# A two-layer transformer in one launch: block attention computes all values first, by rows of tokens, and then queries and keys two units a head

## The chip, the cores and the metric

The kernel runs on one core of one Trainium2 chip. The metric is the time on the device for one launch, in microseconds (us); it was measured in three runs. Besides, one execution was recorded by the profiler, and all durations here come from that one.

## The reference, cut to what matters

The reference is two transformer layers on 512 tokens of width 1024. Each layer is a gated feed-forward block, an attention block and a second feed-forward block, with norms before and after each. The change lies in the attention of the first layer (8 heads of 128). With 512 tokens in two blocks of 256 and every earlier block chosen, its block selection keeps all earlier blocks, so it is plain causal attention:

```
hn  = rms_norm(x, g[2])
qkv = (hn @ w_qkv).reshape(bsz, s_len, 3, A_HEADS, A_HEAD_DIM)     # 1024 x 3072
q   = apply_rope(qkv[:, :, 0], cos_h, sin_h)
k   = apply_rope(qkv[:, :, 1], cos_h, sin_h)
v   = qkv[:, :, 2]
p   = softmax(causal(q @ k.T * 128 ** -0.5))
mix = (p @ v) @ w_o
x   = x + rms_norm(mix, g[3])
```

All data is float32. The kernel keeps float32 accuracy by splitting every operand into a rounded part and a rest (`hi` and `lo`) and by three matmuls for each product: hi x hi, hi x lo, lo x hi.

## The kernel before

The program is written out engine by engine, with semaphores between them; nothing schedules it. Each engine goes strictly through its own list, so an instruction that waits holds up all behind it. TensorE (PE) computes; ScalarE (ACT) makes the hi parts and exponentials; VectorE (DVE) makes the lo parts, the softmax's maxima and normalisation and most evacuations of PSUM; GpSimd (POOL) adds the two halves of the rotary embedding; SyncE (SP) issues the loads of weights.

Weights come as *units* of 1024 x 128 (512 KB) into four slots: a load into `raw`, the hi part `wh` on ACT (`split`, L643), the lo part `wl` on DVE (`split`, L1178), and then 8 tiles of 3 matmuls on PE (`unit`, L1928), which signals `unit_done`. A unit's hi part waits until the unit four places earlier is done.

Activations lie transposed, features on partitions and tokens along the row: `xg` holds the normed input as hi and lo. In stage 1 the attention of the first layer takes 24 units in the order query, key, value of head 0, then of head 1, and so on. The first four units (query, key and value of head 0, query of head 1) are computed by `quad` (L1948): first for tokens 0 to 255, while the second half of `xg` is still being made, and then for tokens 256 to 511, each matmul with 256 columns. In between PE does the transposes for the norms (`mean`, `spread`). All later units have 512 columns.

A value unit gives the head's values transposed. DVE scales them into `tmp` (`evac_v`, L1624), PE turns them back in four 128 x 128 transposes (`value_transposes`, L2168), and `v_split` makes hi and lo parts in `vh` on ACT and DVE. A query or key is evacuated as two products with cosine and sine on DVE (`products`, L1502 and L1503), ACT exchanges the halves (L872), POOL adds, and ACT and DVE make the hi and lo parts (L881, L1507).

For each head `h` from 1 to 6 the loop of PE (L2273) has: the scores of head `h` (`scores`); seven transposes of the probabilities of head `h - 1` (pieces 0 and 1); the unit 3h+4; three more transposes (piece 2); the unit 3h+5; probabilities times values of head `h - 1` (`values`, L2151), whose third step waits until piece 2 has its lo part on DVE; the unit 3h+6; and the value transposes of head `h + 1`. DVE and ACT have their own lists for a head (L1655 and L1004): products, mask, lo parts of the probabilities, maxima, exponentials, normalisation. `out_proj` (L2175) holds the last heads and the first four units of the output projection, whose tiles for the heads already done fill PE meanwhile.

Of the kernel before, what the change touches and what calls it, by code (L numbers as in the profile page):

```python
# [11 lines left out]
P = 128  # L12
# [5 lines left out]
def yoco_kernel(nc: bass.Bass, x, norm_gains, ffn_w1, ffn_w3, ffn_w2, moba_w_qkv, moba_w_o, mla_w_dq,  # L18
# [130 lines left out]
    with ExitStack() as ctx:  # L149
# [129 lines left out]
        def vT_bank(n):  # L279

            return acc[3] if n else aux
# [79 lines left out]
        vT_psum = sem("vT_psum")  # L361
        v_hi = sem("v_hi")
# [52 lines left out]
        def values_of(n):  # L415

            return vh[:, n % 2, 0], vh[:, n % 2, 1]

# [34 lines left out]
        def _(sp):  # L453
# [85 lines left out]
            plain(U0[1], qkv, [HEADS * P * a + P * h for h in range(HEADS) for a in range(3)])  # L539
# [89 lines left out]
        def _(act):  # L629
# [279 lines left out]
            def v_split(n):  # L909
                act.wait_ge(vT_psum, n + 1)  # L910
                s.activation(values_of(n)[0], vT_bank(n)[:].rearrange("p (t d) -> p t d", d=P), COPY
                             ).then_inc(v_hi, 1)
# [61 lines left out]
            split(u + 4)  # L974
            split(u + 5)
            load_table(EXP)
            split(u + 6)
            split(u + 7)

            def exchanged(h, i):  # L980
                exchange(evacuated, r + 3 * h + i + 1, (rope_q, rope_k)[i])
# [6 lines left out]

            probT_zeros()
            for i in range(2):  # L990
                exchanged(0, i)
            for i in range(2):
                rotated(0, i)
            v_split(0)

            for i in range(2):
                exchanged(1, i)
            for i in range(2):
                rotated(1, i)
            softmax_exp(0)  # L1000
            v_split(1)
            split(u + 8)
            split(u + 9)
            for h in range(1, HEADS - 1):  # L1004
                exchanged(h + 1, 0)
                probT_split(h - 1, (0, 1))
                rotated(h + 1, 0)
                split(u + 3 * h + 7)
                if h == 1:
                    probT_split(h - 1, (2,))  # L1010
                softmax_exp(h)
                exchanged(h + 1, 1)
                if h > 1:
                    probT_split(h - 1, (2,))
                split(u + 3 * h + 8)
                rotated(h + 1, 1)
                o_split(h - 1)
                split(u + 3 * h + 9)
                v_split(h + 1)
            probT_split(HEADS - 2, (0, 1, 2))  # L1020
            softmax_exp(HEADS - 1)
            o_split(HEADS - 2)
# [147 lines left out]
        def _(dve):  # L1170
# [391 lines left out]
            def v_split(n):  # L1562
                dve.wait_ge(v_hi, n + 1)
                v_h, v_l = values_of(n)
                v.tensor_tensor(v_l, vT_bank(n)[:].rearrange("p (t d) -> p t d", d=P), f32(v_h),
# [58 lines left out]
            def evac_v(u_count, bank):  # L1624
                dve.wait_ge(unit_done, u_count)
                v.tensor_tensor(T[3][:], bank, Rb[:], ALU.mult).then_inc(evacuated, 1)

            def products(h, i):
                if h:
                    dve.wait_ge(part_lo, 2 * (h - 1) + i + 1)  # L1630
                rope_products(u + 3 * h + i + 1, att_banks[1][3 * h + i][:], cosR, sinR, (rope_q, rope_k)[i])
# [4 lines left out]
            products(0, 0)  # L1636
            products(0, 1)
            split(u + 6)
            evac_v(u + 3, acc[2][:])
            rotated(0, 0)  # L1640
            rotated(0, 1)
            products(1, 0)
            products(1, 1)
            split(u + 7)
            v_split(0)
            softmax_mask(0)
            softmax_max(0)
            evac_v(u + 6, att_banks[1][5][:])
            rotated(1, 0)
            rotated(1, 1)  # L1650
            softmax_norm(0)
            v_split(1)
            split(u + 8)
            split(u + 9)
            for h in range(1, HEADS - 1):  # L1655
                products(h + 1, 0)
                softmax_mask(h)
                probT_split(h - 1, (0, 1))
                softmax_max(h)
                rotated(h + 1, 0)  # L1660
                split(u + 3 * h + 7)
                if h == 1:
                    probT_split(h - 1, (2,))
                softmax_norm(h)
                products(h + 1, 1)
                if h > 1:
                    probT_split(h - 1, (2,))
                split(u + 3 * h + 8)
                rotated(h + 1, 1)
                o_split(h - 1)  # L1670
                split(u + 3 * h + 9)
                evac_v(u + 3 * h + 6, att_banks[1][3 * h + 5][:])
                v_split(h + 1)
            probT_split(HEADS - 2, (0, 1, 2))
            softmax_mask(HEADS - 1)
            softmax_max(HEADS - 1)
            softmax_norm(HEADS - 1)
            o_split(HEADS - 2)
# [197 lines left out]
        def _(pe):  # L1876
# [70 lines left out]

            def quad(st, xg0, n_post, n_pre, between=None):  # L1948
# [168 lines left out]
            def scores(n, rope=None):  # L2117
                if n:
                    pe.wait_ge(exp_ready, TS * n)
                for c in range(TS):  # L2120
                    if n == 0 and c == TS - 1:

                        pe.wait_ge(evacuated, R0[1] + 5)
# [13 lines left out]
            def prob_transposes(n, pieces):  # L2137
                pe.wait_ge(prob_ready, TS * (n + 1))
                for b in pieces:
                    if b == 1 and (n + 1) % HEADS:  # L2140
                        pe.wait_ge(v_lo, n + 2)
# [9 lines left out]
            def values(n):  # L2151

                if n:
                    pe.wait_ge(o_lo, n)
                else:
                    pe.wait_ge(evacuated, R0[1] + 7)
                pe.wait_ge(v_lo, n + 1)
# [10 lines left out]
            def value_transposes(n, r_count):  # L2168
                pe.wait_ge(evacuated, r_count)
                for j in range(TS):  # L2170
                    ins = t.transpose(vT_bank(n)[:, j * P:(j + 1) * P],
                                      (T[3] if n < HEADS else Rb)[:, j * P:(j + 1) * P], ident[:])
                ins.then_inc(vT_psum, 1)

            def out_proj(st, u, r, n, heads, last_scores):  # L2175
# [14 lines left out]
                pe.wait_ge(evacuated, att - 1)  # L2190
                pe.wait_ge(o_lo, last - 2)
                heads_done(0, 0, HEADS - 3)
                value_transposes(last, att)
                prob_transposes(last - 1, (0,))
                last_scores()
                prob_transposes(last - 1, (1,))
                pe.wait_ge(o_lo, last - 1)
                heads_done(0, HEADS - 3, HEADS - 2)
                prob_transposes(last - 1, (2,))
                pe.wait_ge(evacuated, att)  # L2200
                heads_done(1, 0, HEADS - 2)
                values(last - 1)
# [57 lines left out]
            quad(1, XG0[X_F0], N_F0, N_PRE1)  # L2260

            def qkv_unit(rr):
                unit(u + rr, att_dst(1, rr), from_x(xg))


            qkv_unit(4)
            qkv_unit(5)
            value_transposes(0, r + 3)
# [4 lines left out]
            for h in range(HEADS - 1):  # L2273
# [122 lines left out]
```

## Time and profile before

| | us |
|---|---|
| median of three runs (1861.65, 1863.51, 1863.53) | 1863.51 |
| the profiled execution | 1861.66 |
| its span, first to last instruction | 1859.7 |
| PE busy | 1842.6 |
| DVE busy | 1318.0 |
| ACT busy | 914.3 |
| POOL busy | 53.6 |

The busy times are of the span. A row of a matmul gives its full time through the array, which overlaps with the next one; what a matmul costs in a dense stretch is the distance between two starts. The granted clock of TensorE is given as a share of full speed, and is 1.00 in every stretch of this execution. The attention of the first layer lies between 364 us and 567 us.

### The profile page before, as it was taken

How to read it: one execution, taken by the hardware profiler on the slowest of the kernel's cores; microseconds unless marked ns; L12 is line 12 of the kernel's file. 1: busy time of each engine (PE TensorE's matmuls, PEld its weight loads, DVE VectorE, ACT ScalarE, POOL GpSimd, SP SyncE). 2: the span in 40 equal slices, each digit the busy share in tenths (PEclk: the TensorE clock that was granted, in tenths of full speed). 3: DMA queues.
4: the chain of work that ended last, by engine and by line, in shares of the span. 5: the costliest groups of instructions: out<-in, count | busy, mean ns of one | idle time of the engine just before them, and what ended most of it. 6: DMA issues, size and time to landing. Idle time of an engine off the chain costs nothing.

```text
span 1859.7 us, 31170 instructions
## 1 busy us (share of the span) xinstructions
PE 1842.6 (99%) x12175; PEld 1693.9 (91%) x12175; DVE 1318.0 (71%) x1742; ACT 914.3 (49%) x1386; POOL 53.6 (3%) x51
## 2 busy tenths in 40 slices
PE   8999999999999999999999999999999999999999
PEld 7899988988889899998898999989988898999888
DVE  6888862487656888882288888822888488888623
ACT  6455552355545545562255555622666464455522
POOL 0000000011100000000000000000000000000000
PEclk9999999999999999999999999999999999999999
DMA  6244343232223333333323343333221232343331
GB/s 183 80 113 113 91 115 102 79 90 72 77 57 102 91 91 106 97 104 106 108 57 108 91 113 104 102 98 104 63 63 57 69 91 84 99 112 105 109 102 47
DMA packets 339464, 174.64 MB, mean 94 GB/s; under 512 B 11070, under 2 KB 337836, under 8 KB 339372
## 3 DMA queue, kind: packets, MB, share of 16 engines
q1 hardware_dynamic: 338656, 172.25, 33.0%
q8 instruction: 65, 1.06, 0.2%
q10 hardware_dynamic: 716, 1.11, 0.2%
q14 instruction: 27, 0.22, 0.0%
HBM read 171.24 MB, written 2.10 MB: 93 GB/s over the span
## 4 chain that ended last, share of the span: by engine, by line
PE 85%; DVE 9%; ACT 3%; issue 2%; DMA 0%; POOL 0%; DVEq 0%; SPq 0%; ACTq 0%
PE acc L1881 19%; PE acc L1882 19%; PE acc L1883 19%; PE duo L1881 9%; PE duo L1883 9%; PE duo L1882 9%; DVE wl L1175 2%; DVE xg L1220 1%; DVE mx L1534 1%; PE acc L2147 1%; DVE probT L1555 1%; ACT prob L889 1%; DVE y L1240 1%; ACT wh L641 0%; DVE xT L1247 0%
## 5 line engine op out<-in xcount | busy, mean ns | idle before, releaser
L1881 PE MATMUL acc<-xg,wh 128*128 128x256 f32 (+1 forms) x1040 | 340.4, 327 | 2.4 <-DVE xg L1220 1.0
L1883 PE MATMUL acc<-xg,wl 128*128 128x256 f32 (+1 forms) x1040 | 336.9, 324 | 0.0
L1882 PE MATMUL acc<-xg,wh 128*128 128x256 f32 (+1 forms) x1040 | 336.8, 324 | 0.0
L1175 DVE TENSOR_TENSOR wl<-raw,wh 128x1024 fp32r<-128x1024 f32 (+2 forms) x198 | 228.9, 1168 | 126.5 <-ACT wh L641 126.2
L1882 PE MATMUL acc<-hT,wh 128*128 128x512 f32 (+1 forms) x704 | 255.2, 363 | 0.0
L1881 PE MATMUL acc<-hT,wh 128*128 128x512 f32 (+1 forms) x704 | 255.2, 363 | 0.0
L1883 PE MATMUL acc<-hT,wl 128*128 128x512 f32 (+1 forms) x704 | 255.2, 362 | 0.0
L641 ACT ACTIVATE wh<-raw 128x1024 fp32r<-128x1024 f32 (+2 forms) x198 | 194.4, 1011 | 116.4 <-PE acc L1883 71.8
L1881 PEld LDWEIGHTS acc<-xg,wh 128*128 128x128 f32 x1040 | 197.7, 190 | 20.5 <-issue 3.1
L1883 PEld LDWEIGHTS acc<-xg,wl 128*128 128x128 f32 x1040 | 197.7, 190 | 15.8
L1882 PEld LDWEIGHTS acc<-xg,wh 128*128 128x128 f32 x1040 | 197.9, 190 | 14.9
L730 ACT ACTIVATE tmp<-tmp 128x512 f32<-128x512 f32 x88 | 55.5, 631 | 225.6 <-DVE tmp L1437 130.9
L775 ACT ACTIVATE wh<-raw 128x1024 fp32r<-128x1024 f32 x128 | 134.7, 1055 | 48.7 <-PE duo L1883 47.9
L1881 PEld LDWEIGHTS acc<-hT,wh 128*128 128x128 f32 x704 | 132.9, 189 | 20.7
L1883 PEld LDWEIGHTS acc<-hT,wl 128*128 128x128 f32 x704 | 132.9, 189 | 20.6
L1882 PEld LDWEIGHTS acc<-hT,wh 128*128 128x128 f32 x704 | 132.9, 189 | 20.5
L1881 PE MATMUL duo<-xg,wh 128*128 128x256 f32 (+1 forms) x528 | 151.5, 287 | 0.0
L1882 PE MATMUL duo<-xg,wh 128*128 128x256 f32 (+1 forms) x528 | 151.1, 286 | 0.0
L1883 PE MATMUL duo<-xg,wl 128*128 128x256 f32 (+1 forms) x528 | 151.1, 286 | 0.0
L1407 DVE TENSOR_TENSOR wl<-raw,wh 128x1024 fp32r<-128x1024 f32 x128 | 150.9, 1217 | 0.2 <-ACT wh L775 0.2
L1881 PE MATMUL duo<-tx,wh 128*128 128x256 f32 x512 | 144.9, 283 | 0.0
L1882 PE MATMUL duo<-tx,wh 128*128 128x256 f32 x512 | 144.9, 283 | 0.0
(283 smaller groups left out, 4175.6 us busy)
## 6 DMA issues: line engine op xcount, KB each, us to landing
raw<-in_ffn_w_dram SPq DMA_DIRECT2D x238, 512.0 KB, 4.2
raw<-in_ffn_w_dram SPq DMA_DIRECT2D x32, 384.0 KB, 3.4
raw<-in_moba_w_qkv_dram SPq DMA_DIRECT2D x24, 512.0 KB, 3.8
raw<-in_moba_w_o_dram SPq DMA_DIRECT2D x8, 512.0 KB, 3.8
raw<-in_mla_w_o_dram SPq DMA_DIRECT2D x8, 512.0 KB, 3.7
xin<-in_x_dram SPq DMA_DIRECT2D x4, 512.0 KB, 5.4
raw<-in_mla_w_dq_dram SPq DMA_DIRECT2D x4, 512.0 KB, 3.9
raw<-in_mla_w_uq_dram SPq DMA_DIRECT2D x8, 256.0 KB, 2.9
```

The costliest lines, as they stand in the source:

```text
L641: s.activation(wh[:, slot, 0:tiles], raw[:, slot, 0:tiles], COPY).then_inc(w_hi, 1)
L730: s.activation(T[1][:], src, SILU).then_inc(silu_ready, 1)
L775: s.activation(dst, src, COPY).then_inc(w_hi, 1 + (i == 2))
L889: s.activation(prob_of(n, c), sco[bank][:, o:o + (c + 1) * P], EXP, bias=nmx[:, c:c + 1], scale=A_SCALE if n < HEADS else qscale[:, c:c + ...
L1175: v.tensor_tensor(wl[:, slot, 0:tiles], raw[:, slot, 0:tiles], f32(wh[:, slot, 0:tiles]), ALU.subtract).then_inc(w_lo, 1)
L1220: v.scalar_tensor_tensor(out=dst[:, 1, m, cols], in0=xT[:, m, cols], scalar=gains[:, gcol + m:gcol + m + 1], in1=f32(dst[:, 0, m, cols]), ...
L1240: v.tensor_tensor(y[:, a:b, half(e)], y[:, a:b, half(e)], norm_bank[e][:, half(e)].unsqueeze(1).broadcast_to([P, b - a, HALF]), ALU.mult). ...
L1407: v.tensor_tensor(dst, src, f32(high), ALU.subtract).then_inc(w_lo, 1 + (i == 2))
L1534: ins = v.tensor_reduce(mx[:, c:c + 1], sco[bank][:, o:o + (c + 1) * P], AX_X, ALU.max)
L1881: t.matmul(dst, w_h, m_h, start=start, stop=False, skip_group_check=onto)
L1882: t.matmul(dst, w_h, m_l, start=False, stop=False, skip_group_check=onto)
L1883: return t.matmul(dst, w_l, m_h, start=False, stop=stop, skip_group_check=onto)
```

## The change

Two things change in stage 1, and no others.

The eight value units are computed first, for all heads, and by rows of tokens: a matmul now takes 128 tokens of `xg` as its stationary operand and 512 columns of the value weights, four heads, as its moving one (`values_product`). The result has tokens on partitions, as `values` wants it, and no transposes are left. A unit now holds two of the eight feature tiles for four heads, loaded in one DMA. `all_values` does heads 0 to 3 for token blocks 0 and 1, then 2 and 3, and heads 4 to 7 in the same way. The results lie in all eight PSUM banks, four at a time; ACT writes the hi part with the token's norm factor as its scale (`values_hi`), DVE the lo part in one instruction (`values_lo`), both into `oT`, where each head's output later takes the place of its values.

After that come queries and keys, two units a head, for heads 0 and 1 before the first scores and then two heads ahead. The loop of a head has two units instead of three. The lists of ACT and DVE for a head are written anew, and `out_proj` has a form of its own for this stage (`moba_heads`), into which heads 5 to 7 fall.

```diff
-        for st, special in ((1, {4: sco[2], 5: acc[0], 6: aux}), (5, {KQ: sco[1], KQ + 1: sco[2]})):
+        for st, special in ((1, dict(enumerate((*acc, *sco, aux, *acc)))), (5, {KQ: sco[1], KQ + 1: sco[2]})):
...
+            def values_product(dst, slot, k, c, start, stop):
+                (x_h, x_l), cols = from_x(xg, slice(c * P, (c + 1) * P))(k), slice(VG * (k % 2), VG * (k % 2 + 1))
+                dst = dst[:].rearrange("p (h d) -> p h d", d=P)
+                t.matmul(dst, x_h, wh[:, slot, cols], start=start, stop=False)
+                t.matmul(dst, x_h, wl[:, slot, cols], start=False, stop=False)
+                return t.matmul(dst, x_l, wh[:, slot, cols], start=False, stop=stop)
+
+            def all_values(xg0, n_post, n_pre):
...
+                for e in range(2):
+                    for k in range(KD):
+                        if e == 0:
+                            pe.wait_ge(w_lo, u + k // 2 + 1)
+                        pe.wait_ge(xg_ready, xg0 + KD * e + k + 1)
+                        for c in range(HT * e, HT * (e + 1)):
+                            ins = values_product(att_banks[1][c], k // 2, k, c, k == 0, k == KD - 1)
...
+                        if (e, k) == (1, 4):
+                            mean(n_pre)
+                        if (e, k) == (1, 7):
+                            spread(n_pre)
...
 PE, the loop over heads:
-            for h in range(HEADS - 1):
+            for h in range(2):
+                qk_unit(h, 0)
+                qk_unit(h, 1)
+            for h in range(HEADS - 2):
                 moba_scores(h)
                 if h:
                     prob_transposes(h - 1, (0, 1))
-                    qkv_unit(3 * h + 4)
+                qk_unit(h + 2, 0)
+                if h:
                     prob_transposes(h - 1, (2,))
-                    qkv_unit(3 * h + 5)
                     values(h - 1)
-                if h + 2 < HEADS:
...
-                    qkv_unit(3 * h + 6)
-                if h + 2 < HEADS:
-                    value_transposes(h + 1, r + 3 * h + 6)
+                qk_unit(h + 2, 1)
...
+                def moba_heads():
+                    last_scores(last - 1)
+                    prob_transposes(last - 2, (0, 1))
...
+                    heads_done(0, 0, HEADS - 4)
+                    prob_transposes(last - 2, (2,))
+                    values(last - 2)
...
+                    heads_done(1, 0, HEADS - 4)
+                    last_scores(last)
+                    prob_transposes(last - 1, (0, 1))
+                    pe.wait_ge(o_lo, last - 1)
+                    heads_done(0, HEADS - 4, HEADS - 2)
+                    prob_transposes(last - 1, (2,))
+                    values(last - 1)
+                    heads_done(1, HEADS - 4, HEADS - 2)
```

The new list of ACT for a head (the removed lines have the old order, with three units a head):

```diff
+            for h in range(HEADS):
+                if h:
+                    probT_split(h - 1, (0, 1))
+                if h + 1 < HEADS:
+                    for i in range(2):
+                        rotated(h + 1, i)
+                softmax_exp(h)
+                if h:
+                    probT_split(h - 1, (2,))
+                for i in range(2):
+                    if h + 2 < HEADS:
+                        exchanged(h + 2, i)
+                    if i and h:
+                        o_split(h - 1)
+                    if h + 1 < HEADS:
+                        split(u + 14 + 2 * h + i)
```

And the new list of DVE for a head:

```diff
+            for h in range(HEADS):
                 softmax_mask(h)
+                if h:
+                    probT_split(h - 1, (0, 1))
                 softmax_max(h)
+                if h + 1 < HEADS:
+                    for i in range(2):
+                        rotated(h + 1, i)
+                softmax_norm(h)
+                if h:
+                    probT_split(h - 1, (2,))
+                for i in range(2):
+                    if h + 2 < HEADS:
+                        products(h + 2, i)
+                    if i and h:
+                        o_split(h - 1)
+                    if h + 1 < HEADS:
+                        split(u + 14 + 2 * h + i)
```

On PE, the place is behind the three transposes of piece 2 of a head. Before, a whole unit (24 matmuls from `xg`) stood there; here are its first rows:

```order
1829 L2147 MATMUL acc<-ident,prob_odd_104 128x128 x3
1830 L1881 MATMUL acc<-xg,wh 128x512
1831 L1882 MATMUL acc<-xg,wh 128x512
1832 L1883 MATMUL acc<-xg,wl 128x512
1833 L1881 MATMUL acc<-xg,wh 128x512
```

After the change the product of probabilities and values (`probT` and the values in `oT`) follows at once:

```order
1800 L2210 MATMUL acc<-ident,prob 128x128 x3
1801 L1899 MATMUL duo<-probT,oT 128x512
1802 L1900 MATMUL duo<-probT,oT 128x512
1803 L1901 MATMUL duo<-probT,oT 128x512
1804 L1899 MATMUL duo<-probT,oT 128x384
1805 L1900 MATMUL duo<-probT,oT 128x384
1806 L1901 MATMUL duo<-probT,oT 128x384
1807 L1899 MATMUL duo<-probT,oT 128x256
```

The unit that stood between has moved away: of a head's three units one lies ahead of the transposes and one behind the product.

On DVE, the place is the stretch ahead of a head's mask (the instruction on `duo` with `mask`) and behind it. `wl` is the lo part of a weight unit, `rope_k` and `tmp` the rotary products, `oT<-duo` the lo part of a head's output. Before, for a head in the middle:

```order
254 L1175 TENSOR_TENSOR wl<-raw,wh 128x1024
255 L1507 TENSOR_TENSOR kh<-rope_k_102,kh 128x512
256 L1560 TENSOR_TENSOR oT<-duo,oT 128x512
257 L1175 TENSOR_TENSOR wl<-raw,wh 128x1024
258 L1626 TENSOR_TENSOR tmp_64<-acc,Rb 128x512
259 L1565 TENSOR_TENSOR vh<-acc,vh 128x512
260 L1502 TENSOR_TENSOR tmp_62<-acc,sinR 128x512
261 L1503 TENSOR_TENSOR tmp_61<-acc,cosR 128x512
262 L1525 TENSOR_TENSOR duo<-duo,mask 128x128 x4
263 L1555 TENSOR_TENSOR probT<-acc,probT 128x512
```

And now:

```order
236 L1523 TENSOR_TENSOR rope_k_101<-acc,sinR 128x512
237 L1524 TENSOR_TENSOR rope_k_102<-acc,cosR 128x512
238 L1581 TENSOR_TENSOR oT<-duo,oT 128x512
239 L1196 TENSOR_TENSOR wl<-raw,wh 128x1024
240 L1546 TENSOR_TENSOR duo<-duo,mask 128x128 x4
241 L1576 TENSOR_TENSOR probT<-acc,probT 128x512
242 L1576 TENSOR_TENSOR probT<-acc,probT 128x384
243 L1555 TENSOR_REDUCE mx<-duo 128x1 x4
```

The products of the key's unit, which is the last one ahead of the scores on PE, now stand ahead of the mask, and the output's and one unit's lo part stand between the two.

## Rows read from the trace of the kernel before

**Rows 1.** The page: busy share of PE, and its granted clock in 40 slices.

```profile
PE 1842.6 (99%) x12175; PEld 1693.9 (91%) x12175; DVE 1318.0 (71%) x1742; ACT 914.3 (49%) x1386; POOL 53.6 (3%) x51
...
PEclk9999999999999999999999999999999999999999
```

**Rows 2.** Timeline of PE: start, duration, instruction; a 512-column matmul, then 256.

```profile
566.60 0.39 PE L1883 MATMUL duo<-oT,wl 128*128 128x512 f32 x1
566.83 0.28 PE L1881 MATMUL acc<-oT,wh 128*128 128x256 f32 x1
566.94 0.28 PE L1882 MATMUL acc<-oT,wh 128*128 128x256 f32 x1
```

**Rows 3.** Timeline of PE over one head of the loop (h = 5).

```profile
496.99 0.60 PE L2171 MATMUL acc<-ident,tmp 128*128 128x128 f32 x4
...
499.36 0.93 PE L2147 MATMUL acc<-ident,prob 128*128 128x128 f32 x7
...
505.59 0.49 PE L2147 MATMUL acc<-ident,prob 128*128 128x128 f32 x3
...
511.39 0.39 PE L1881 MATMUL duo<-probT,vh 128*128 128x512 f32 x1
...
512.63 0.38 PE L1881 MATMUL duo<-probT,vh 128*128 128x256 f32 x1
...
513.45 0.40 PE L1881 MATMUL acc<-xg,wh 128*128 128x512 f32 x1
...
518.90 0.60 PE L2171 MATMUL acc<-ident,tmp 128*128 128x128 f32 x4
```

**Rows 4.** Timeline of DVE over one head (h = 4).

```profile
476.91 0.68 DVE L1502 TENSOR_TENSOR tmp<-acc,sinR 128x512 f32<-128x512 f32 x1
...
478.11 0.88 DVE L1525 TENSOR_TENSOR duo<-duo,mask 128x128 f32<-128x128 f32 x4
480.23 1.15 DVE L1555 TENSOR_TENSOR probT<-acc,probT 128x512 fp32r<-128x512 f32 x2 [1.24 <-ACT probT L897]
481.30 1.67 DVE L1534 TENSOR_REDUCE mx<-duo 128x1 f32<-128x128 f32 x4
483.01 0.17 DVE L1539 TENSOR_SCALAR nmx<-mx 128x4 f32<-128x4 f32 x1
...
485.40 0.18 DVE L1546 RECIPROCAL rsums<-psums 128x4 f32<-128x4 f32 x1 [0.49 <-ACT prob L889]
485.61 1.27 DVE L1549 TENSOR_SCALAR prob<-prob,rsums 128x128 f32<-128x128 f32 x4
...
490.01 0.62 DVE L1555 TENSOR_TENSOR probT<-acc,probT 128x256 fp32r<-128x256 f32 x2 [1.93 <-ACT probT L897]
```

**Rows 5.** Timeline of ACT over the same head.

```profile
478.23 1.28 ACT L872 ACTIVATE tmp<-tmp 64x512 f32<-64x512 f32 x2 [1.95 <-DVE tmp L1503]
...
483.22 0.37 ACT L889 ACTIVATE prob<-duo,nmx 128x128 f32<-128x128 f32 x1 [0.72 <-DVE nmx L1539]
...
485.15 0.21 ACT L889 ACTIVATION_READ_ACCUMULATOR prob<-duo,nmx 128x1 f32 x1
...
491.71 0.60 ACT L907 ACTIVATE oT<-duo 128x512 fp32r<-128x512 f32 x1 [0.26 <-PE duo L1883]
492.21 1.06 ACT L641 ACTIVATE wh<-raw 128x1024 fp32r<-128x1024 f32 x1
```

**Rows 6.** Timeline of DVE: last square sum of the norm before attention.

```profile
383.97 0.42 DVE L1295 SCALAR_TENSOR_TENSOR sqs<-sqs 128x256 f32<-128x256 f32 x1
```

**Rows 7.** Timeline of PE at the program's start.

```profile
6.05 1.09 PE L2249 MATMUL duo<-ident,xin 128*128 128x128 f32 x4 [6.05 <-DMA xin<-in_x_dram]
...
7.11 2.77 PE L2249 MATMUL duo<-ident,xin 128*128 128x128 f32 x12
10.89 0.36 PE L1881 MATMUL acc<-xg,wh 128*128 128x256 f32 x1 [1.01 <-DVE xg L1220]
```

**Rows 8.** Windows: busy time (count) by engine, granted clock, DMA share, GB/s.

```profile
8.00:10.00 2.00, 1.88 (x9) 1.48 (x7) 1.67 (x4) 1.79 (x4) 0.00 (x0) 1.00 1.11 358
```

More of the change, by code:

```diff
@@ L415, in values_of, with values_part @@
         def values_of(n):
+            if n < HEADS:
+                return tuple(oT[:, a, n].rearrange("p (t d) -> p t d", d=P) for a in range(2))
             return vh[:, n % 2, 0], vh[:, n % 2, 1]
+        def values_part(i, a):
+            g, c = divmod(i, TS)
+            return oT[:, a, VG * g:VG * (g + 1), c * P:(c + 1) * P]
         def o_of(n, a):
@@ L538, in _ @@
             qkv = kpn(moba_w_qkv[0])
-            plain(U0[1], qkv, [HEADS * P * a + P * h for h in range(HEADS) for a in range(3)])
+            for i in range(V_UNITS):
+                g, j = divmod(i, KD // 2)
+                slot_free(U0[1] + i)
+                sp.dma_start(raw[:, i % SLOTS].rearrange("p (k h) n -> p k (h n)", k=2),
+                             qkv[:, 2 * j:2 * j + 2, (2 * HEADS + VG * g) * P:(2 * HEADS + VG * (g + 1)) * P]
+                             ).then_inc(raw_full[i % SLOTS], 16)
+            plain(U0[1] + V_UNITS, qkv, [HEADS * P * a + P * h for h in range(HEADS) for a in range(2)])
             plain(U0[1] + 3 * HEADS, kpn(moba_w_o[0]), range(0, D, P))
@@ L987, in rotated @@
                 part((qh, kh)[i][:, 0], (rope_q, rope_k)[i][1][:])
+            split(u + 4)
+            split(u + 5)
+            load_table(EXP)
+            for i in range(TS):
+                values_hi(i)
+            split(u + 6)
+            split(u + 7)
+            for i in range(TS, TS + HT):
+                values_hi(i)
+            for w in range(8, 11):
+                split(u + w)
             probT_zeros()
+            for i in range(TS + HT, 2 * TS):
+                values_hi(i)
+            split(u + 11)
             for i in range(2):
@@ L1630, in products @@
                     dve.wait_ge(part_lo, 2 * (h - 1) + i + 1)
-                rope_products(u + 3 * h + i + 1, att_banks[1][3 * h + i][:], cosR, sinR, (rope_q, rope_k)[i])
+                rope_products(u + V_UNITS + 2 * h + i + 1, att_banks[1][V_RES + 2 * h + i][:], cosR, sinR,
+                              (rope_q, rope_k)[i])
             def rotated(h, i):
                 part(2 * h + i, (qh, kh)[i], (rope_q, rope_k)[i][1])
-            products(0, 0)
-            products(0, 1)
+            for i in range(TS):
+                values_lo(i)
@@ new lines, in _ @@
+            for i in range(TS, TS + HT):
+                values_lo(i)
+            for w in range(8, 11):
+                split(u + w)
+            for i in range(TS + HT, 2 * TS):
+                values_lo(i)
+            split(u + 11)
+            for i in range(2):
+                products(0, i)
+            for i in range(2):
+                rotated(0, i)
+            for i in range(2):
+                split(u + 12 + i)
+                products(1, i)
+            for h in range(HEADS):
@@ L1669, in _ @@
[L1669 to L1678, printed above, removed]
+                if h + 1 < HEADS:
+                    for i in range(2):
+                        rotated(h + 1, i)
@@ L1679, in _ @@
+                softmax_norm(h)
+                if h:
+                    probT_split(h - 1, (2,))
+                for i in range(2):
+                    if h + 2 < HEADS:
[4 more added lines that the diff above has]
+                        split(u + 14 + 2 * h + i)
             probT_split(HEADS - 1, (0, 1, 2))
@@ L2259, in _, with qk_unit @@
             u, r = U0[1], R0[1]
[L2260 to L2268, printed above, removed]
+            all_values(XG0[X_F0], N_F0, N_PRE1)
+            def qk_unit(h, i):
+                rr = V_RES + 2 * h + i
+                unit(u + V_UNITS + 2 * h + i, att_dst(1, rr), from_x(xg))
             def moba_scores(h):
```

169 lines of the change are left out of this document (79 added, 90 removed).

## The prediction

> **What bounds the kernel now.** I read the page first: PE is busy for 99% of the span, at a granted clock of full speed in all slices [rows 1]. Nothing that shortens another engine's work can help by itself. The change has to take work from PE, and it must not make PE wait. So the second view is PE's timeline. In a dense stretch a 512-column matmul costs 0.227 us from start to start (0.23 in the row) and a 256-column one 0.12, so two halves cost slightly more than one whole [rows 2]. A 128x128 transpose costs 0.11: seven take 0.93 and four 0.60, and the difference is three of them [rows 3].
>
> One head of the loop takes 518.90 - 496.99 = 21.91 us without a gap [rows 3]. Its parts: value transposes with the change of shape 0.44; scores 1.93 (to 499.36); seven transposes 0.77; a unit 5.46; three transposes 0.33 (from 505.59); a unit 5.47; probabilities times values 2.06 (511.39 to 513.45); a unit 5.45. The third view is the timeline of DVE and ACT over a head, which tells how long the softmax takes from scores to normalised probabilities. These engines idle now and then, which costs nothing while PE has a unit in hand.
>
> **PE's own work.** The value units keep their 192 matmuls of 512 columns, with the operands' roles swapped; I take 0.227 for them too. `quad`'s 192 halves (four units x 8 tiles x 3 x 2) become 96 whole: 192 x 0.12 - 96 x 0.227 = 1.2 us less. The eight groups of four value transposes go: 8 x 0.44 = 3.5 us less [rows 3]. Together -4.7 us. The 32 lo and hi parts of values are off PE's path.
>
> **The value stage.** `mean` for the norm ahead of attention stood behind 24 + 12 halves of the second token half in the order before; now it stands behind five feature tiles, that is 5 x 6 x 0.227 = 6.8 us, and the first half is 0.6 us shorter. PE comes to it at about 383.4. DVE's last square sum ends at 383.97 + 0.42 = 384.39 [rows 6], and DVE's chain up to there is not moved: 1.0 us of waiting. Later, the third unit of heads 4 to 7 gets its lo part behind the norm's factors, both tables and four `values_lo` on DVE, about 395.3: the norm's factors come to DVE when PE is through the first group, 389.6, then 0.7 + 2 x 0.6 for factors and tables, 4 x 0.6 for the lo parts, 1.13 for the unit and some 0.2 of handing over. PE wants it after four feature tiles of the second group, 389.5 + 5.4 = 394.9: 0.4 us. Some 0.3 us of waits of that kind are there before, so I book +1.1.
>
> **A head in the new loop.** Without waits it would take 21.91 - 5.45 - 0.44 = 16.0 us. But DVE and ACT have a chain that is longer than PE's cover. I count from t = 0, where PE ends the key's unit and starts the scores of head h. The durations are those of rows 4 and 5, an op of 512 columns on DVE counting 0.60 to the next one (two from 476.91 to 478.11).
> - The key's two products on DVE: PE's end is seen 0.2 later, then 0.60 + 0.68: to 1.5. Before, the mask had only a query's products ahead of it, whose unit had ended long before.
> - ACT exchanges the halves (1.28): to 2.8. Then the output's hi part, which follows it in ACT's list (0.49 to the next [rows 5]), to 3.3; the unit's hi part, 1.06: to 4.4.
> - DVE's lo part of that unit, 1.13: to 5.5. The mask, 0.93: to 6.5 (scores were ready at 2.1, so all that stands ahead of it counts).
> - Lo parts of the earlier head's pieces 0 and 1, 1.07 (480.23 to 481.30): to 7.5. Maxima 1.71: to 9.25. Scaled maxima, then ACT's exponentials, from 483.01 to 483.22 to 485.36: 2.35, to 11.6.
> - Reciprocal and normalisation, 485.40 to 486.80: 1.4, to 13.0. Lo part of piece 2, 0.62 [rows 4]: to 13.65.
>
> PE comes to that piece much earlier. Scores, seven transposes, the query's unit and three transposes take 8.5 us; the first two steps of `values` (511.39 to 512.6, [rows 3]) 1.2: PE stands at 9.7 before the third step and can start it at about 13.75. That is a wait of 4.05 us in every head. Before, a whole unit of 5.47 us lay between the three transposes and `values` and hid it, and in DVE's list the lo part of piece 2 came at 490.01, just in time even so. Behind PE's wait stand the rest of `values` (0.8) and the key's unit (5.45), whose end starts the next head's chain, so nothing is won back: a head takes 20.0 us instead of 16.0. The pattern holds for h = 1 to 5 (h = 0 has no `values`): 5 x 4.05 = +20.2 us.
>
> **The last heads.** For head 6 the scores, seven transposes, half of one output tile (12 matmuls, 2.7 us instead of a unit's 5.4), three transposes and two steps bring PE to 7.0; the chain is the same, 13.75: 6.7 us. For head 7 nothing stands ahead of the mask. Counted from the start of its scores: scores 1.9, mask, lo parts, maxima, exponentials, normalisation and piece 2 take up to 10.7; PE's own work (scores, transposes, 6 matmuls of the output projection 1.4, three transposes, two steps) is done at 5.8: 4.9 us. Some 0.3 of small waits are there before. Together +11.3.
>
> **Sum.** -4.7 + 1.1 + 20.2 + 11.3 = +27.9 us.
>
> **The clock after a wait.** This is the cost that the trace of before hardly shows, since there PE waits longer than 1.01 us only at the start. After 6.05 us without work PE's twelve transposes took 2.77 us, which is (2.77 - 0.27) / 11 = 0.227 each instead of 0.11; then, after a wait of 1.01 us, 256-column matmuls went at full pace from 10.89 on [rows 7]. The window's granted clock reads 1.00 all the same [rows 8], so half speed may hide behind that figure. Sixteen transposes at twice their price make 1.9 us. A wait of 6.7 us is longer than the one that showed this, so I count one such loss, +2.0. Those of 4.05 and 4.9 lie between 1.01 and 6.05; nearest is the 6.05, but for these I take nothing in the sum and keep 6 x 2.0 = 12 us for the range; at the low end the clock costs nothing anywhere. The Trainium skill, in "TensorE: Matmul & The Clock Gate", section "HAM oscillation — how this bites in real kernels", says that a recurring idle gap in front of matmuls throws the clock back to half at every turn of a loop. The row at the program's start agrees with it as far as it goes; no row here shows it within the loop. By that rule each of the seven waits would be paid a second time, which is the second rival below.
>
> So the sum is 1861.66 + 27.9 + 2.0 = 1891.5 us against the profiled execution's own time. The median before is 1.85 us higher than that time, within the spread of its three runs.
>
> **Other edits.** The value loads have the same bytes in longer pieces; no weight is waited for in the loop now, and a head of the new loop needs two units in 20 us instead of three in 22, so the loads and the SP queue are not late. Cost nothing, at most the 0.4 us already booked. ACT's hi parts of values wait for token factors; DVE behind them has 5 us before a unit of its is wanted. If that cover failed, one unit's lo part (1.1 us) would be late once.
>
> **Rivals.**
> 1. *The same chain, but shorter.* The mask may not stand behind all I put there, for instance if ACT's part of output and unit is done before the key's products (it isn't by the list). From 2.1 instead of 5.5 the chain would end at 10.3: waits of 0.6 in five heads, 3.3 in head 6 and 4.9 in head 7: -4.7 + 1.1 + 3.0 + 3.3 + 4.6 = +7.3, 1869. For it speaks that DVE is busy for only 71%; against it that the list is strictly in order.
> 2. *Every wait also costs clock*: 1891.5 + 12 = 1903.5. For it: the first matmuls of the program. Against it: 4.05 is shorter than 6.05.
> 3. *Faster*: PE isn't held at the third step of `values`, because the softmax of a head goes on while the key's unit still runs (a single mechanism: piece 2's parts overtaking the normalisation). Then only PE's work counts: -4.7, 1857. It decides from the point where the lo part of piece 2 is there by 9.7 us of a head. Both lists have it behind the exponentials and the normalisation, so this would need the chain to lose 4 us.
> 4. *The value stage costs much more*: swapped operands read with another stride might cost as much as two halves, 0.24 instead of 0.227, +2.5; if all four units of a group waited for DVE, some +4: 1898.
>
> **Chances.** The forecast (its waits, and the clock lost once or twice) 0.55, its own range 1885 to 1897; rival 1: 0.13; rival 2: 0.17; rival 3: 0.05; rival 4: 0.10. The range of 8 in 10 runs from 1880 (waits of 2.5 instead of 4.05, no clock lost) to 1904. What can be told from no change is 0.2%, 3.7 us. Faster beyond that needs rival 3: 0.04; within it 0.03; slower 0.93.
>
> **What would show it.** In the profile after: the busy share of PE falls below 99% and the waits of PE name `probT` from DVE with some 4 us, five times or more, the longest nearly 7; the distance between two heads' scores is 20 us and not 16; nothing waits on loads; the transposes of values are gone; a wait of 1 us stands at `mean` ahead of attention. Matmuls right behind a long wait at twice the usual distance would show the clock. I am wrong if PE reaches the third step of `values` and finds its piece there.

## The result: 1906.0 us, slower by 2.3%, and the profile after

The changed kernel took 1906.02 us (median of four, 1905.08 to 1906.43) against 1863.47 for the kernel before. The ratio is 1.023, with a 95% interval of 1.0212 to 1.0248. The forecast was 1891.5 and its range ended at 1904: the direction was right, the time was not.

The page of the profiled execution (1905.08 us, span 1903.1): busy time by engine, PE's granted clock in 40 slices of 47.6 us, and who holds the chain that ended last.

```profile
PE 1854.4 (97%) x12047; PEld 1697.8 (89%) x12047; DVE 1316.2 (69%) x1734; ACT 913.1 (48%) x1386; POOL 52.8 (3%) x51
...
PEclk9999999999888999999999999999999999999999
...
PE 83%; DVE 11%; ACT 3%; issue 2%; DMA 0%; POOL 0%; DVEq 0%; SPq 0%; ACTq 0%
```

Beside [rows 1] two things stand out. PE has 128 matmuls and transposes fewer and is nevertheless busy for longer (1854.4 against 1842.6 us), and the clock has fallen in the slices from 476 to 618 us, where the heads are. DVE holds 11% of the chain that ended last (9% before).

The waits of PE between 355 and 625 us: who waits for whom, us in total, times, longest.

```profile
PE duo L1899 <- DVE probT L1576: 29.3, 7, 4.7
PE acc L2210 <- DVE probT L1576: 1.8, 1, 1.8
PE duo L1928 <- DVE sqs L1316: 0.8, 1, 0.8
PE duo L1970 <- DVE wl L1196: 0.5, 1, 0.5
```

The seven waits for piece 2 of the probabilities are there, one for each of heads 0 to 6. So are the two small ones of the value stage. Now the head h = 2, from its scores to the next ones, on PE's timeline (start, duration, instruction, in brackets the idle time and what ended it). It answers to [rows 3].

```profile
468.76 0.28 PE L1899 MATMUL duo<-kh,qh 128*128 128x256 f32 x1
...
478.33 0.34 PE L1901 MATMUL duo<-probT,oT 128*128 128x384 f32 x1
482.54 0.58 PE L1899 MATMUL duo<-probT,oT 128*128 128x256 f32 x1 [3.87 <-DVE probT L1576]
...
484.41 0.63 PE L1900 MATMUL acc<-xg,wh 128*128 128x512 f32 x1
484.83 0.63 PE L1901 MATMUL acc<-xg,wl 128*128 128x512 f32 x1
...
488.52 0.40 PE L1901 MATMUL acc<-xg,wl 128*128 128x512 f32 x1
488.75 0.40 PE L1899 MATMUL acc<-xg,wh 128*128 128x512 f32 x1
...
491.51 0.28 PE L1899 MATMUL duo<-kh,qh 128*128 128x256 f32 x1
```

Two losses follow each other. PE idles for 3.87 us in front of the third step of `values`. Then the matmuls come at half pace: 484.83 - 484.41 = 0.42 us from start to start, and from 488.52 on 0.23 again, the pace of [rows 2]. From one head's scores to the next it is 491.51 - 468.76 = 22.75 us. The five heads of the loop took 22.27, 22.75, 21.66, 22.72 and 21.64, which is 22.2 on average, where the head with its wait and without any clock loss was worked out as 20.05.

The same head in windows of 5 us (length; busy time and count of PE, PEld, DVE, ACT, POOL; granted clock; DMA share, GB/s):

```profile
475.00:480.00 5.00, 3.66 (x19) 2.80 (x17) 4.38 (x11) 1.82 (x8) 0.00 (x0) 1.00 0.36 105
480.00:485.00 5.00, 2.46 (x9) 2.27 (x10) 3.18 (x9) 2.13 (x6) 0.00 (x0) 0.65 0.00 0
485.00:490.00 5.00, 5.00 (x17) 3.92 (x16) 1.32 (x1) 1.06 (x1) 1.28 (x1) 0.67 0.25 73
490.00:495.00 5.00, 5.00 (x31) 4.41 (x30) 1.29 (x2) 1.84 (x4) 0.53 (x1) 1.00 0.12 35
```

A clock of 0.65 to 0.67 is a window in which part of the time was at the lower of the two levels (1.2 GHz) and part at the upper one (2.4 GHz). From 485 to 490 PE is full, with 17 matmuls where the same window at full clock has 27 (experiment 1). This is why its busy time went up.

DVE's timeline of the same head answers to [rows 4]:

```profile
469.64 0.68 DVE L1524 TENSOR_TENSOR rope_k<-acc,cosR 128x512 f32<-128x512 f32 x1
472.29 0.69 DVE L1581 TENSOR_TENSOR oT<-duo,oT 128x512 fp32r<-128x512 f32 x1 [1.98 <-ACT oT L920]
473.24 1.23 DVE L1196 TENSOR_TENSOR wl<-raw,wh 128x1024 fp32r<-128x1024 f32 x1 [0.25 <-ACT wh L654]
474.38 0.89 DVE L1546 TENSOR_TENSOR duo<-duo,mask 128x128 f32<-128x128 f32 x4
475.30 1.16 DVE L1576 TENSOR_TENSOR probT<-acc,probT 128x512 fp32r<-128x512 f32 x2
476.37 1.67 DVE L1555 TENSOR_REDUCE mx<-duo 128x1 f32<-128x128 f32 x4
...
480.68 1.27 DVE L1570 TENSOR_SCALAR prob<-prob,rsums 128x128 f32<-128x128 f32 x4
481.87 0.61 DVE L1576 TENSOR_TENSOR probT<-acc,probT 128x256 fp32r<-128x256 f32 x2
```

Taken from the start of the scores at 468.76 the chain is the one that was counted: key's products done at 1.6 (counted 1.5), mask begun at 5.6 (5.5), maxima done at 9.3 (9.25), normalisation done at 13.2 (13.0), piece 2 done at 13.7 (13.65). PE's third step starts at 482.54 - 468.76 = 13.78 (13.75).

### The profile page after: what moved, and what is told of

The parts are those of the page before. It is cut to its first block, busy times and chain, and to the rows that moved or that the text cites. A ratio compares the mean times of both kernels' runs of the same rounds, so it can differ in the third digit from the quotient of the medians.

```text
span 1903.1 us, 30919 instructions
## 1 busy us (share of the span) xinstructions
PE 1854.4 (97%) x12047; PEld 1697.8 (89%) x12047; DVE 1316.2 (69%) x1734; ACT 913.1 (48%) x1386; POOL 52.8 (3%) x51
## 3 DMA queue, kind: packets, MB, share of 16 engines
q1 hardware_dynamic: 332512, 172.25, 31.9%
## 4 chain that ended last, share of the span: by engine, by line
PE 83%; DVE 11%; ACT 3%; issue 2%; DMA 0%; POOL 0%; DVEq 0%; SPq 0%; ACTq 0%
PE acc L1899 18%; PE acc L1900 18%; PE acc L1901 18%; PE duo L1899 9%; PE duo L1900 9%; PE duo L1901 9%; DVE wl L1196 1%; DVE xg L1241 1%; DVE mx L1555 1%; DVE probT L1576 1%; ACT wh L654 1%; ACT prob L902 1%; DVE y L1261 1%; DVE xT L1268 1%; ACT prob_odd L902 0%
## 5 line engine op out<-in xcount | busy, mean ns | idle before, releaser
L1899 PE MATMUL acc<-xg,wh 128*128 128x256 f32 (+1 forms) x960 | 318.8, 332 | 2.2 <-DVE xg L1241 1.0
L1900 PE MATMUL acc<-xg,wh 128*128 128x256 f32 (+1 forms) x960 | 315.6, 329 | 0.0
L1901 PE MATMUL acc<-xg,wl 128*128 128x256 f32 (+1 forms) x960 | 315.0, 328 | 0.0
L1899 PEld LDWEIGHTS acc<-xg,wh 128*128 128x128 f32 x960 | 184.6, 192 | 20.4 <-issue 2.8
L1901 PEld LDWEIGHTS acc<-xg,wl 128*128 128x128 f32 x960 | 184.4, 192 | 15.9
L1900 PEld LDWEIGHTS acc<-xg,wh 128*128 128x128 f32 x960 | 184.7, 192 | 15.1
L1899 PE MATMUL duo<-xg,wh 128*128 128x256 f32 x512 | 145.4, 284 | 0.0
L1900 PE MATMUL duo<-xg,wh 128*128 128x256 f32 x512 | 145.1, 283 | 0.0
L1901 PE MATMUL acc<-tx,wl 128*128 128x256 f32 x512 | 145.1, 283 | 0.0
L1900 PE MATMUL duo<-tx,wh 128*128 128x256 f32 x512 | 145.1, 283 | 0.0
L1899 PE MATMUL acc<-tx,wh 128*128 128x256 f32 x512 | 145.1, 283 | 0.0
```

What stands on the lines that cost most here:

```text
L1899: t.matmul(dst, w_h, m_h, start=start, stop=False, skip_group_check=onto)
L1900: t.matmul(dst, w_h, m_l, start=False, stop=False, skip_group_check=onto)
L1901: return t.matmul(dst, w_l, m_h, start=False, stop=stop, skip_group_check=onto)
```

## The experiments

Each ran beside the kernel before on the same chip, which took 1863.03 us there for experiments 1, 3 and 4 and the kernel with 17 transposes, and 1861.96 us for the one with 8 and experiment 5. "Waits" are those of PE from 355 to 625 us. A slow stretch is a run of matmuls behind a wait at about half pace (512 columns 0.43 us apart, 256 columns 0.21). Its loss is what they take beyond 0.227 and 0.12, less the 0.1 us that the first one behind a wait takes longer at full clock too.

### 1. The wait filled with idle work

```
 for j in range(TS):                                      # values(n), on PE
+    if j == 2 and n < HEADS - 1:
+        for i in range(34):
+            t.transpose(acc[3][:, i % TS * P:(i % TS + 1) * P], ident[:], ident[:])
     if j < 3: pe.wait_ge(probT_lo, 3 * n + j + 1)
```

> The changed kernel with 34 transposes of the identity into a free PSUM bank in front of the third step of values for heads 0 to 6: PE works 3.7 us in the place where it waits now; nothing reads what they write. Clock theory (the slow stretch behind each wait is the clock that fell while PE stood still): the heads keep their length but for the slow stretch, 20.0 us instead of 22.2 on average, matmuls at 0.227 us throughout, about 1889 to 1892 in all. Rival (the slow stretch comes from something else, such as memory access of ACT and DVE beside it): it stays, 1905, or grows if the transposes come on top.

Measured: 1889.62 us, ratio 1.0142 (1.0125 to 1.0159). PE computes 7 x 34 transposes more, which nobody reads, and the kernel is 16.4 us faster than the changed one. PE's timeline and windows of the same head:

```profile
478.90 3.87 PE L2226 MATMUL acc<-ident 128*128 128x128 f32 x34
482.94 0.39 PE L1899 MATMUL duo<-probT,oT 128*128 128x256 f32 x1 [0.17 <-DVE probT L1576]
483.16 0.28 PE L1900 MATMUL duo<-probT,oT 128*128 128x256 f32 x1
```

```profile
480.00:485.00 5.00, 4.83 (x38) 4.38 (x37) 3.18 (x9) 2.14 (x8) 0.00 (x0) 1.00 0.00 0
485.00:490.00 5.00, 5.00 (x27) 4.26 (x26) 1.84 (x2) 1.46 (x2) 1.30 (x1) 1.00 0.15 41
```

The third step starts no earlier, since the piece comes when it comes. But there is no slow stretch, the clock is 1.00, and a head takes 20.08 us. So the slow stretch is due to PE's idling, and to nothing else that the change did. From the first scores to the end of the first four output tiles the changed kernel takes 610.13 - 433.65 = 176.48 us and this one 596.56 - 435.56 = 161.0: the clock cost 15.5 us, 2.2 a wait. What is left agrees with the sum without the clock, 1861.66 + 27.9 = 1889.6.

### 2. The wait filled in part

The same edit with 17 and with 8 transposes.

> As the kernel with 34 transposes, but with 17 (1.9 us of work), so that about 2.1 us of waiting are left in each head. If waits of 2 us still cost the clock: slow stretches of 0.43 us a matmul stay, about 1902 to 1905. If they don't: about 1890, like the one with 34. Waits of 0.84 us cost nothing in the changed kernel, waits of 3.9 us do; this lies between.

> As the kernels with 34 and 17 transposes, but with 8 (0.9 us of work), so that about 3 us of waiting are left in each of the five heads, and 3.7 us at heads 5 and 6. With 17 transposes waits of 2.0 us cost the clock in one head of five and those of 2.7 to 2.8 us in two of three; with none, waits of 3.9 and more always. If the chance grows with the length, most of these seven cost it: 1898 to 1904. If 2.8 us and more were the same as 3.9, all: 1905.

Measured: with 17, 1893.9 us (1891.09 to 1895.69), ratio 1.016 (1.0143 to 1.0177); with 8, 1904.21 (two runs, 1902.29 and 1906.14), 1.0225 (1.0207 to 1.0244). With 8 the waits were 3.63 us in the first head, four of 2.98 to 3.01, 3.78 and 3.8, with slow stretches behind the first six (some 13 us together) and none behind the last. With 17 they were 2.67, four times 2.02, 2.80 and 2.81. Two of those of 2.02, each with the next matmul:

```profile
502.31 0.39 PE L1899 MATMUL duo<-probT,oT 128*128 128x256 f32 x1 [2.02 <-DVE probT L1576]
502.54 0.28 PE L1900 MATMUL duo<-probT,oT 128*128 128x256 f32 x1
...
522.38 0.42 PE L1899 MATMUL duo<-probT,oT 128*128 128x256 f32 x1 [2.02 <-DVE probT L1576]
522.60 0.41 PE L1900 MATMUL duo<-probT,oT 128*128 128x256 f32 x1
```

One wait of 2.02 us cost nothing, and an equal one 20 us later brought a slow stretch. Of the four of 2.02 only this one did, the 2.67 did not, 2.80 and 2.81 did. So below 3 us it isn't the length alone that decides. With 17 the time lies between the two outcomes that I had put down. The kernel's own executions differ in the same way: 1895.69, 1895.43, 1892.38 and 1891.09 us go with a granted clock, averaged over the whole execution, of 0.997, 0.997, 0.998 and 0.999. In the profiled one (1895.69) the three slow stretches cost 4.5 us and a slow start of the program (see the last section) 1.3; without them it would be at 1889.9, close to the time with 34.

### 3. The order of `values` alone, in the kernel before

```
     prob_transposes(h - 1, (2,))
-    qkv_unit(3 * h + 5)
     values(h - 1)
+    qkv_unit(3 * h + 5)
```

> The kernel before with one move: the product of probabilities and values stands directly behind the three transposes of piece 2, ahead of the value unit, as in the changed kernel; all else is as before. Theory A: PE reaches the third step at 9.7 us of a head, the piece has its lo part at 15.1 us there: a wait of 5.4 us in six heads and a slow stretch of 2.2 us behind each, +32 +13 = about 1907. Theory B (the place is harmless and the loss comes from two units instead of three or from the values by rows): within 5 us of before.

Measured: 1903.85 us, ratio 1.022 (1.0203 to 1.0237). One line moved in the kernel before costs 40.8 us, nearly as much as the whole change (42.6). Its wait in one head:

```profile
509.19 0.58 PE L1881 MATMUL duo<-probT,vh 128*128 128x256 f32 x1 [5.33 <-DVE probT L1555]
```

Five such waits and a first one of 2.68 make 29.3 us, and all six are followed by a slow stretch (8 to 17 matmuls, 12.0 us together): 29.3 + 12.0 = 41.3, and between the two profiled executions lie 1902.83 - 1861.66 = 41.2 us. The new value stage, the swapped operands and the missing transposes aren't in this kernel. It isn't they that cost; what costs is that no unit stands any more between piece 2's transposes and its use.

### 4. `values` behind the key's unit, in the changed kernel

```
     prob_transposes(h - 1, (2,))
-    values(h - 1)
     qk_unit(h + 2, 1)
+    values(h - 1)
```

(and likewise `values(last - 2)` behind its output tile)

> The changed kernel with one move on PE: the product of probabilities and values stands behind the head's second unit again instead of in front of it (and, for head 5, behind the tile of the output projection). Theory A (the waits come from that place: PE reaches the third step of values at 9.7 us of a head, the piece is there at 13.75, and each such wait also costs 2.2 us of half-speed matmuls): PE gets there at 15 us, so five waits of 4 us and their slow stretches go, head 5's shrinks to about 2 us, head 6's (4.7 us) stays: 1861.7 - 4.7 + 1.1 + 2 + 4.9 + 2 to 4 = about 1867 to 1869, and 16.0 us from one head's scores to the next. Theory B (the softmax chain of ACT and DVE is the bound of a head, wherever PE stands): 20 us a head as before, above 1888.

Measured: 1881.41 us, ratio 1.0099 (1.0083 to 1.0116), some 13 us over what I expected. The wait at the third step is gone from the loop, but a head takes 18.3 us and not 16. The waits are now these; the longest of the first row (3.9 us, in front of head 5's three transposes, where I had expected about 2) and of the second (4.7) bring a slow stretch each:

```profile
PE acc L2210 <- DVE probT L1576: 9.0, 6, 3.9
PE duo L1899 <- DVE probT L1576: 5.2, 2, 4.7
PE acc L1899 <- DVE wl L1196: 4.1, 5, 0.8
```

DVE's timeline of this kernel, over one round of a head:

```profile
466.56 0.68 DVE L1524 TENSOR_TENSOR rope_k<-acc,cosR 128x512 f32<-128x512 f32 x1
469.21 0.69 DVE L1581 TENSOR_TENSOR oT<-duo,oT 128x512 fp32r<-128x512 f32 x1 [1.98 <-ACT oT L920]
470.16 1.23 DVE L1196 TENSOR_TENSOR wl<-raw,wh 128x1024 fp32r<-128x1024 f32 x1 [0.25 <-ACT wh L654]
471.30 0.89 DVE L1546 TENSOR_TENSOR duo<-duo,mask 128x128 f32<-128x128 f32 x4
...
479.91 0.68 DVE L1524 TENSOR_TENSOR tmp<-acc,cosR 128x512 f32<-128x512 f32 x1
483.03 1.34 DVE L1196 TENSOR_TENSOR wl<-raw,wh 128x1024 fp32r<-128x1024 f32 x1 [2.44 <-ACT wh L654]
...
484.89 0.68 DVE L1524 TENSOR_TENSOR rope_k<-acc,cosR 128x512 f32<-128x512 f32 x1
```

One round of DVE's list takes 484.89 - 466.56 = 18.33 us. In this round DVE waits for ACT alone and ACT for DVE alone, neither for PE. Twice in it DVE stands for about 2 us, because ACT first exchanges the halves of what DVE has just computed and only then makes the hi part that DVE's next instruction needs. The strict order of the two lists sets a second limit of 18.3 us, which my expectation had left out. PE meets it as 0.75 to 0.84 us at the query's unit and 1.16 at the three transposes.

### 5. Other lists for DVE and ACT

On both engines, written here for DVE (ACT's list is changed in the same places):

```
     softmax_max(h)
+    if h in (1, 2, 3, 4, 5, 7): split(u + 13 + 2 * h)
     rotated(h + 1, 0); rotated(h + 1, 1)
+    if 1 < h < 7: o_split(h - 2)
+    if h > 5: probT_split(h - 1, (2,))
     softmax_norm(h)
-    if h: probT_split(h - 1, (2,))
-    for i in range(2):
-        products(h + 2, i)
-        if i and h: o_split(h - 1)
-        split(u + 14 + 2 * h + i)
+    if 0 < h < 6: probT_split(h - 1, (2,))
+    products(h + 2, 0)
+    split(u + 14 + 2 * h)
+    products(h + 2, 1)
+    if h == 5: split(u + 25)
+    if h > 5: o_split(h - 1)
```

A unit's and the output's lo part go from in front of the mask to behind the maxima, where DVE would wait for the exponentials anyway. First with PE's order as in the changed kernel:

> The changed kernel with PE's order as it is (values in front of the head's second unit) and new lists for ACT and DVE alone: the lo part of a weight unit and the head's output come behind the maxima instead of ahead of the mask, a unit's hi part behind the first pieces on ACT, and for the last two heads piece 2 comes ahead of the exponentials. Theory (the chain counted instruction by instruction): the mask starts at 2.15 us of a head instead of 5.5, piece 2 is there at 11.2 instead of 13.65, so five waits of 1.6 us instead of 4.05, too short to cost the clock, and 2.3 and 1.2 us at the last heads: 1861.7 - 4.7 + 1.1 + 8 + 3.5 = 1870. Rival (the chain is set by something else, exponentials and transposes): waits stay near 4 us, 1895 or more.

Measured: 1876.72 us (three runs, 1876.69 to 1877.96; a fourth took 6146.59, is left out and has no explanation here), ratio 1.0081 (1.0063 to 1.0099). That is 29 us faster than the changed kernel by the lists alone, though I had expected 1870. PE's waits:

```profile
PE duo L1917 <- DVE oT L1590: 6.9, 5, 3.4
PE duo L1917 <- DVE probT L1585: 5.8, 6, 2.1
```

The first row is a wait that I made myself. The output's lo part now frees its PSUM half later than `values`, unmoved, wants it: 0.86 us in four heads and 3.44 in head 5. There are slow stretches behind only two waits: the 3.44 and the first for the piece (2.00). Behind the latter the slow pace starts late:

```profile
458.55 0.39 PE L1917 MATMUL duo<-probT,oT 128*128 128x256 f32 x1 [2.00 <-DVE probT L1585]
458.77 0.28 PE L1918 MATMUL duo<-probT,oT 128*128 128x256 f32 x1
...
459.84 0.63 PE L1919 MATMUL acc<-xg,wl 128*128 128x512 f32 x1
460.27 0.63 PE L1917 MATMUL acc<-xg,wh 128*128 128x512 f32 x1
...
562.59 0.39 PE L1917 MATMUL duo<-probT,oT 128*128 128x256 f32 x1 [2.07 <-DVE probT L1585]
```

Eight matmuls start at full pace before it. Behind the 2.07 of the last row nothing is slow at all.

Then the new lists with `values` late, as in experiment 4, and with `values(last - 1)` too behind its output tile:

> The same new lists, and on PE values behind the head's second unit, as in the first experiment, and both parts of head 5 and 6's output tiles ahead of the last values. The first experiment took 18.3 us a head, for a wait on a weight unit (0.8) and on the first piece's lo part (1.2), both held up by DVE's list. Theory: with the work behind the maxima both go, a head takes 16.0 us, and all that is left is PE's own saving of 4.7 us less 1.1 of the value stage and some 1.5 at the end: 1859 to 1861. If the round through DVE's list is longer than 16 us, 17 us a head and 1865.

Measured: 1862.74 us (eleven runs, 1860.87 to 1863.02), ratio 1.0 (0.9991 to 1.0009), where I had expected 1859 to 1861. A head takes 15.92 us, the 16.0 of the prediction's head without waits. That is 43.3 us less than the changed kernel: of the waits for the piece 0.7 is left, 0.7 for the output's lo part, and 1.9 in front of head 5's three transposes.

And with the value stage's two small waits attacked too, the transposes for the mean one feature tile later and a unit's split between the parts of the values:

```
-    if (e, k) == (1, 4): mean(n_pre)
+    if (e, k) == (1, 5): mean(n_pre)
-    for i in range(TS): values_lo(i)          # hi likewise on ACT
-    split(u + 6)
+    for i in range(2): values_lo(i)
+    split(u + 6)
+    for i in range(2, TS): values_lo(i)
```

> The kernel just ahead with two more moves in the value stage: the mean of the norm ahead of attention stands one feature tile later on PE, and the third unit of heads 4 to 7 is split between the second and the third of the values' parts on ACT and DVE. Theory: the waits of 0.84 and 0.54 us measured there go: 1.3 us less than the kernel just ahead, 1858 to 1860, and so faster than the kernel before.

Measured: 1859.27 us (eleven runs, 1859.1 to 1861.78), ratio 0.9985 (0.9976 to 0.9994). This version beats both kernels, the one before by 2.7 us. Against the version ahead of it the median fell by 3.5 us and the fastest execution by 1.8, where the two waits that are gone were 1.4; the rest is not shown and lies within the spread of the single executions (2.2 and 2.7 us). Against the page of the changed kernel PE has the same instructions and 15.3 us less of busy time:

```profile
PE 1839.1 (99%) x12047; PEld 1687.5 (91%) x12047; DVE 1314.4 (71%) x1734; ACT 914.0 (49%) x1386; POOL 52.9 (3%) x51
```

## Why the prediction was wrong

**The mechanism and the waits: right.** Along the chain the hand count is off by at most 0.2 us, and at the start of PE's third step by 0.03. The waits at the third step were 4.51 for the first head and 3.87 or 3.88 for the others, against 4.05. Those of the last two came with the values of heads 5 and 6 (the prediction names them 6 and 7, after the scores). Head 5's was in two pieces, 1.76 in front of its three transposes (they wait until DVE has made the lo part of piece 0) and 4.65 at the third step, against 6.7 in one. Head 6's was 4.66 against 4.9. All of them make 31.1 us, and 31.9 were counted. Experiment 1, which takes away the clock loss and nothing else, comes to 1889.6: that is the sum of +27.9 us.

**PE's own work and the value stage: right.** The wait at `mean` was 0.85 us (1.0), at the third unit 0.5 (0.4). With all waits of the loop gone the kernel is at 1862.7 and 1859.3 (experiment 5). The latter is 2.3 us above the 1857 that -4.7 alone would give, and has 3.4 us of waits left in the heads.

**The clock after a wait: wrong, and it is the step that failed.** The prediction says: "A wait of 6.7 us is longer than the one that showed this, so I count one such loss, +2.0", and for those of 4.05 and 4.9 "I take nothing in the sum". In fact all seven waits at the third step were followed by 11 to 17 matmuls at half pace. Their losses are 1.6 to 2.8 us each and 15.6 altogether. The term was 2.0 and should have been 15.6; the sum with it is 1861.66 + 27.9 + 15.6 = 1905.2, and 1905.08 was measured. The price of one loss (1.9 to 2.0) was a little low, 2.2 on average; its number, one instead of seven, was wrong. My own argument ran the other way: for a wait between 1.01 and 6.05 us the nearest row was the 6.05, which I had read as showing the loss, and still I put it at nothing. The price itself came from a row that shows something else. In [rows 7] PE goes at half pace from its very first transpose, so that the clock had not risen yet; it wasn't lost by a wait, and the wait of 1.01 us was no test of one either (last section). That 2.0 lies near the measured 2.2 is luck. (The distance in that row is 0.21 us too and not 0.227, since the last transpose takes 0.42 and not 0.27.) The Trainium skill, in "TensorE: Matmul & The Clock Gate", section "HAM oscillation — how this bites in real kernels", says that an idle gap which is long enough and comes back at every turn of a loop throws the clock back every time. This trace agrees, seven times in seven, for waits from 3.87 to 4.66 us. It was rival 2, with a chance of 0.17, and the 8-in-10 range ended 2 us below the time.

**The rivals.** Rival 1 (shorter chain) and 3 (faster) had no share: the list is kept strictly. Rival 4 had none either: the 192 value matmuls, with swapped operands, stand 0.227 us apart in the median.

## What to carry to other kernels

Where a list moves a consumer ahead of independent work on PE, count the producer's whole chain on the other engines in the order of their lists; here it was right to 0.2 us over a chain of 13.7. Then price each new wait of PE twice, once for itself and once for the matmuls behind it: here 1.3 to 2.8 us for nearly every wait from 2.8 us on, also inside a loop that is otherwise full. And ask how long one round of the other engines' lists takes by itself: taking a wait away on PE helps only down to that length, and here the lists alone were worth 29.3 us, PE's order alone 24.6, and both together 43.3.

## What the runs showed of the hardware

The loss after a wait is no steady function of its length. Waits of PE of 0.5 to 1.2 us within the heads were never followed by a slow stretch, and seven of 1.4 to 2.0 us in front of head 5's transposes weren't either. At the third step of `values` a slow stretch followed two of six waits of 2.0 to 2.1 us (experiments 2 and 5), one of two at 2.67 and 2.68, and all six at 2.80 to 3.01. From 3.4 us on, wherever they stood, it followed all but one (the last of 3.8 us in the kernel with 8 transposes). The price varies as well where the wait does not: of the changed kernel's four waits of 3.87 or 3.88 us two cost 2.7 us and two 1.6, in turn, which is why its heads take 22.7 and 21.7 us in turn. What decides this is not shown.

At the program's start the clock comes up sooner in some executions than in others. The profiled execution of experiment 1 took 1891.53 us, its other three 1889.5 to 1889.7. Its timeline of PE at the place of the last of [rows 7]:

```profile
10.98 0.55 PE L1899 MATMUL acc<-xg,wh 128*128 128x256 f32 x1 [1.02 <-DVE xg L1241]
11.33 0.42 PE L1900 MATMUL acc<-xg,wh 128*128 128x256 f32 x1
...
14.96 0.36 PE L1899 MATMUL acc<-xg,wh 128*128 128x256 f32 x1
```

Behind the same wait of 1.0 us, where the execution of before went on at full pace, 18 matmuls are 0.21 us apart instead of 0.12: 1.7 us. The wait doesn't cause it. The twelve transposes ahead of it take 2.77 us in both executions, 0.21 each where a transpose costs 0.11 later, so PE was at half pace from its first instruction on. In the profiled execution of the first kernel of experiment 5 the twelve are done sooner, since the last ones go at full pace already:

```profile
7.16 2.50 PE L2355 MATMUL duo<-ident,xin 128*128 128x128 f32 x12
```

So the clock first rose ahead of the wait, during it or up to some 4 us behind it. The slow start shows in the profile of the best version too, which took 1860.91 us where six of its eleven executions took 1859.1 to 1859.3. The executions of the kernel before lie at 1861.65 and at 1863.5, as far apart; that it is for this reason is argued from the others and not shown. The granted clock of 10 to 15 us reads 1.00 in the slow case too, so within the program's first microseconds that figure hides the slow pace, while in the loop (0.65) it shows it. The distance between two starts shows it in both places.
